# Spare words in front of the activations and the feed-forwards' products in SBUF

## The chip, the cores and the metric

The kernel runs on one core of one Trainium2 chip. The metric is the device time of one execution in microseconds (us), taken over several runs; one further execution is recorded by the hardware profiler, and all rows of the trace come from that one. A difference is called measured here when it is over about 0.2% of the time.

## The reference, cut to what matters

Two transformer blocks follow each other on 256 tokens of width 1024, all in float32. The first block has two layers; each has a feed-forward, a mixer and a second feed-forward:

```python
def swiglu(x, w_gate, w_up, w_down):
    return (jax.nn.silu(x @ w_gate) * (x @ w_up)) @ w_down     # 1024 -> 2816 -> 1024
...
for layer in range(2):
    h = h + 0.5 * swiglu(rms_norm(h, ffn1_norm_g[layer]), ...)
    # layer 0: a convolution of 31 taps beside attention to a memory
    # layer 1: causal attention in 12 heads beside attention to a memory
    h = h + concatenate([primary, mem_out]) @ w_o[layer]
    h = h + 0.5 * swiglu(rms_norm(h, ffn2_norm_g[layer]), ...)
```

The second block has one layer: a projection of 1024 to 6664 columns, differential attention, an mLSTM, two output projections that are gated and added, and a last projection. Most of the work of both is the product of 256 rows with weights that are read once.

## The kernel before, in words

**Precision.** A float32 product is made of three products of a rounded type (fp32r). Each weight tile is split by ACT into a rounded part `whi` (line 1295) and by DVE into the rest `wlo` (line 1897); activations are split in the same way into `xh` and `xl`, and the feed-forward's products into `gh` and `gl`. What is summed is hi by hi, lo by hi and hi by lo.

**Layout.** `B.x` holds two buffers `x0` and `x1`, each [128, 8, 2, 256]: for each of the 8 chunks of the width, 256 tokens of `xh` and behind them 256 tokens of `xl`. `F.g` of the four feed-forwards, `g0` to `g3`, is [128, 22, 2, 256] in the same manner. So one matmul can stream 512 columns, hi and lo, from one chunk.

**Products.** TensorE runs one long program. All matmuls go through the helper `mm` (line 505). In the feed-forwards and most projections a weight tile of 128 by 128 is the stationary operand and the activation moves; `block` makes two matmuls of each:

```python
def block(b, h, l, x, start, stop, ready=None):
    mm(bank[b], h, x.rearrange("p a b -> p (a b)"), start, False)      # 512 columns: hi and lo by whi
    ...
    return mm(bank[b][:, 0:S], l, x[:, 0, :], False, stop)             # 256 columns: hi by wlo
```

`part` and `cols` call it for the gate and up columns, for 8 chunks of `x`; `down` calls it for the 22 chunks of `g`, for 4 pairs of output columns and 2 columns in each: 176 times in each feed-forward. `direct` and `pair` serve the other projections with products of 256 columns alone, from `xh` twice and `xl` once. `rows_steps` turns it round: the activation is stationary, the weights move in 512 columns, or in 512 and 256 where a tile of weights has 768 columns (`w_kv`).

**Order.** Weights pass through 403 slots in an order written out by hand (`weight_plan`). SyncE loads them into 7 buffers `raw`, ACT and DVE split them 4 slots ahead into 5 buffers of `whi` and `wlo`, TensorE takes them in order. The stages are F0 (0 to 220 us of the trace, with the memory's keys and values inside it), mixer A (to 315), F1 (to 525), F2 (to 710), mixer B (to 837), F3 (to 1014), and the second block. F0, F2 and F3 read `x0`, F1 reads `x1`. In each, gate and up columns come first and the 22 chunks of `g` last. ACT copies the right halves of the sums out of PSUM (line 1342) and rounds them (1440); DVE adds, scales and subtracts (1971, 2055, 2063, 2067).

**Where the tensors lie.** Buffers are taken from a stack (`buffers`): those of the whole program first, then each stage's on top, which later stages reuse. In the built program of before they start at these bytes of a partition:

```
raw 16512   whi 45184   wlo 65664   gcol 103552 (256 bytes)
x0 103808   x1 120192   ident 136576   ...   htmp 158528   memt 162624
g0 174912   g1 162624   g2 175392   g3 162624
taps 165696 (840 bytes)   tapp 166560
cs 174912 (128)   posi 175040 (8)   posf 175072 (8)   freq 175104 (32)   ang 175136   rd 175264
```

`g2` lies on top of the keys and values of mixer B (`kT` to `rd`), which F2 must leave alone.

Of the kernel before, what the change touches and what calls it, by code (L numbers as in the profile page):

```python
# [6 lines left out]
F32 = mybir.dt.float32  # L7
# [185 lines left out]
def buffers(nc, ctx):  # L193
# [3 lines left out]
    def sb(name, shape, dt=F32, c=ctx):  # L197
        return c.enter_context(nc.sbuf_tensor(name, shape, dt))
# [9 lines left out]
    B.rowr = sb("rowr", [128, 2, S])  # L208
    B.diag = sb("diag", [128, 2, 128])
    B.gcol = sb("gcol", [128, 8, 8])  # L210
    B.x = [sb(f"x{i}", [128, 8, 2, S], F32R) for i in range(2)]
    B.xh = [x[:, :, 0, :] for x in B.x]
    B.xl = [x[:, :, 1, :] for x in B.x]
    B.ident = sb("ident", [128, 128])
# [15 lines left out]
    def ffn_space(f):  # L230
        c = ExitStack()
        F = Space()
        F.g = sb(f"g{f}", [128, 22, 2, S], F32R, c)
        F.gh, F.gl = F.g[:, :, 0, :], F.g[:, :, 1, :]
        F.gr = sb(f"gr{f}", [128, 2, 512], F32, c)
        F.pr = sb(f"pr{f}", [128, 2, 512], F32, c)
        c.close()
        return F

# [7 lines left out]
    B.xn = sb("xn", [128, 2, D], F32, st0)  # L247
    st0.close()
    F0 = ffn_space(0)

    A = B.a = Space()
# [18 lines left out]
    A.ptbuf = A.gr  # L270
    mx.close()
    F1 = ffn_space(1)

    M = B.b = Space()
# [7 lines left out]
    M.ang = sb("ang", [128, 2, 2, 8], F32, kv)  # L282
    M.rd = sb("rd", [128, 2, 2, 8], F32, kv)
    F2 = ffn_space(2)
    mx = ExitStack()
    M.kn = sb("kn", [128, 2, 768], F32, mx)
# [42 lines left out]
def signals(nc, ctx):  # L329
# [3 lines left out]
    def sig(name, events, by=1):  # L333
        return Signal(ctx.enter_context(nc.semaphore(name)), events, by)
# [55 lines left out]
    s.pe_b = sig("pe_mix_b", [("kT", t, i) for t in T2 for i in T2] + [("qT", t, i) for t in T2 for i in T2])  # L390
    s.pe_c = sig("pe_mix_c", ["ctap", "gt", "F"] + [("xrow", t, j) for t in T2 for j in T2])
    s.zo0 = sig("zo_first_tile", range(3))
# [2514 lines left out]
def program(nc, A, out):  # L2907
    with ExitStack() as ctx:
        B = buffers(nc, ctx)
        B.out = out  # L2910
        B.tap_mem = nc.dram_tensor("tap_mem", (128, 192), F32, kind="Internal").ap()
        B.conv_mem = nc.dram_tensor("conv_mem", (3, 2, 128, 32 + S), F32, kind="Internal").ap()
        s = signals(nc, ctx)
        tensor_engine(nc, B, s)
        scalar_engine(nc, B, A, s)
        vector_engine(nc, B, A, s)
        gpsimd_engine(nc, B, s)
        sync_engine(nc, B, A, s)
# [25 lines left out]
```

## Time and profile before

| | us |
|---|---|
| median of 3 runs | 1244.79 (1244.46 to 1245.52) |
| the profiled execution, its own time | 1244.43 |
| its span, first to last instruction | 1242.9 |
| TensorE busy | 1219.7 |
| DVE busy | 882.6 |
| ACT busy | 681.1 |
| GpSimd busy | 60.6 |

The time of the profiled execution and its span differ by 1.5 us, which lie outside the instructions. Matmuls are pipelined: each lasts longer in the trace than the distance to the next, so the pace is read from starts (first and last start of a row with its count), not from the busy time. A row with 176 matmuls has 175 distances. Where windows cut a stretch, the matmul that is running at the window's edge is counted.

### The profile page before, as it was taken

The page shows a single profiled execution, that of the slowest core. Times are in us where ns is not written, and L with a number is a line of the kernel's source. Part 1 is how long each engine was busy: PE and PEld are TensorE (multiplying, and loading weights), DVE is VectorE, ACT ScalarE, POOL GpSimd, SP SyncE. Part 2 cuts the span into 40 slices and gives each one's busy share as a digit, 9 for nine tenths or more (in the row PEclk, how much of TensorE's full clock was granted, in tenths as well). Part 3 has the DMA queues.
Part 4 walks back from the last instruction along what each step waited for, and adds up shares of the span by engine and source line. Part 5 has one row for each costly group of instructions (what it writes and reads, how often), then busy time and mean ns, then how long its engine had stood idle before and what let it go on. Part 6 is the DMA issues. An engine that isn't in the chain of part 4 may idle for free.

```text
span 1242.9 us, 18893 instructions
## 1 busy us (share of the span) xinstructions
PE 1219.7 (98%) x7518; PEld 1070.2 (86%) x7518; DVE 882.6 (71%) x1256; ACT 681.1 (55%) x1032; POOL 60.6 (5%) x89
## 2 busy tenths in 40 slices
PE   7999999989999999999999999999999999999998
PEld 6888888867888888888888888988888899888996
DVE  6686856785787775777775677577776666666875
ACT  5655544543666554565554456656555455556463
POOL 4000100100010000000000122000000000000000
PEclk9999999999999999999999999999999999999999
DMA  8766556672466655666655555047665566556450
GB/s 273 231 203 193 170 182 191 182 212 51 152 195 195 183 182 178 192 184 195 188 182 185 163 175 188 27 129 212 187 200 171 171 190 188 164 142 180 140 173 34
DMA packets 205653, 215.46 MB, mean 173 GB/s; under 512 B 9808, under 2 KB 192592, under 8 KB 205566
## 3 DMA queue, kind: packets, MB, share of 16 engines
q1 hardware_dynamic: 202998, 210.76, 56.9%
q10 hardware_dynamic: 2568, 3.50, 0.8%
q8 instruction: 60, 0.98, 0.3%
q14 instruction: 27, 0.22, 0.1%
HBM read 212.19 MB, written 2.03 MB: 172 GB/s over the span
## 4 chain that ended last, share of the span: by engine, by line
PE 91%; ACT 3%; DVE 3%; issue 2%; DMA 0%; ACTq 0%; POOL 0%; SPq 0%
PE psum L505 89%; ACT whi L1295 1%; DVE wlo L1897 1%; PE psum L669 0%; PE psum L954 0%; DMA xn<-in_x 0%; ACT qn L1599 0%; PE psum L697 0%; ACT qT L1660 0%; ACT L1736 0%; DVE small L2488 0%; ACT zob L1736 0%; ACT pb L1781 0%; ACTq L1410 0%; DVE small L2334 0%
## 5 line engine op out<-in xcount | busy, mean ns | idle before, releaser
L505 PE MATMUL psum<-x,whi 128*128 128x512 f32 (+1 forms) x2288 | 696.2, 366 | 3.5 <-ACT whi L1295 2.4
L1897 DVE TENSOR_TENSOR wlo<-raw,whi 128x1024 fp32r<-128x1024 f32 (+2 forms) x403 | 474.4, 1190 | 187.8 <-ACT whi L1295 184.4
L505 PE MATMUL psum<-x,wlo 128*128 128x256 f32 x1960 | 550.0, 281 | 1.0 <-DVE wlo L1897 1.0
L1295 ACT CAST whi<-raw 128x1024 fp32r<-128x1024 f32 (+2 forms) x403 | 406.1, 1022 | 165.9 <-PE psum L505 156.6
L505 PEld LDWEIGHTS psum<-x,whi 128*128 128x128 f32 x2288 | 409.8, 189 | 77.3 <-ACT whi L1295 2.8
L505 PEld LDWEIGHTS psum<-x,wlo 128*128 128x128 f32 x1960 | 371.8, 190 | 1.6 <-DVE wlo L1897 1.5
L505 PE MATMUL psum<-g,whi 128*128 128x512 f32 x704 | 247.7, 396 | 0.0
L505 PE MATMUL psum<-g,wlo 128*128 128x256 f32 x704 | 197.9, 281 | 0.0
L505 PEld LDWEIGHTS psum<-g,whi 128*128 128x128 f32 x704 | 132.4, 188 | 31.7
L505 PE MATMUL psum<-whi,x 128*128 128x512 f32 (+1 forms) x512 | 141.2, 376 | 0.1
L505 PEld LDWEIGHTS psum<-g,wlo 128*128 128x128 f32 x704 | 132.2, 188 | 0.0
L505 PEld LDWEIGHTS psum<-whi,x 128*128 128x128 f32 x512 | 90.2, 190 | 16.0 <-ACT zob L1708 0.3
L505 PE MATMUL psum<-wlo,x 128*128 128x512 f32 (+1 forms) x256 | 86.5, 373 | 0.0
L1342 ACT COPY pr<-psum 128x512 f32<-128x512 f32 x44 | 25.8, 586 | 67.1 <-PE psum L505 67.0
L1342 ACT COPY gr<-psum 128x512 f32<-128x512 f32 x44 | 25.7, 585 | 61.1 <-PE psum L505 61.1
L1971 DVE TENSOR_TENSOR pr<-psum,pr 128x512 f32<-128x512 f32 x44 | 30.4, 690 | 35.6 <-ACT pr L1342 35.6
L505 PEld LDWEIGHTS psum<-wlo,x 128*128 128x128 f32 x256 | 46.2, 189 | 8.6
L1372 ACT ACTIVATE x<-hT,gcol 128x256 fp32r<-128x256 f32 x64 | 28.5, 500 | 45.3 <-DVE hT L2106 28.8
L1971 DVE TENSOR_TENSOR gr<-psum,gr 128x512 f32<-128x512 f32 x44 | 30.4, 690 | 31.1 <-ACT gr L1342 31.0
L1989 DVE SCALAR_TENSOR_TENSOR x<-hT,gcol,x 128x256 fp32r<-128x256 f32 x64 | 28.8, 498 | 18.2 <-ACT x L1372 18.2
L1431 ACT ACTIVATE gr<-gr 128x512 f32<-128x512 f32 x44 | 27.6, 632 | 21.3 <-DVE gr L2055 21.2
L1440 ACT CAST g<-pr 128x512 fp32r<-128x512 f32 x44 | 27.4, 623 | 19.3 <-DVE pr L2063 19.3
(322 smaller groups left out, 851.3 us busy)
## 6 DMA issues: line engine op xcount, KB each, us to landing
raw<-in_ffn_w_gate SPq DMA_DIRECT2D x88, 512.0 KB, 4.4
raw<-in_ffn_w_up SPq DMA_DIRECT2D x88, 512.0 KB, 4.1
raw<-in_ffn_w_down SPq DMA_DIRECT2D x80, 512.0 KB, 3.8
raw<-in_w_in SPq DMA_DIRECT2D x52, 512.0 KB, 4.1
raw<-in_w_o SPq DMA_DIRECT2D x16, 512.0 KB, 4.7
raw<-in_a_w_in SPq DMA_DIRECT2D x14, 512.0 KB, 4.7
raw<-in_w_kv SPq DMA_DIRECT2D x16, 384.0 KB, 3.3
raw<-in_w_mem_kv SPq DMA_DIRECT2D x8, 512.0 KB, 3.7
```

Source lines behind the costliest of these rows:

```text
L505: return pe.matmul(o, l, r, start=start, stop=stop, skip_group_check=True)
L1295: act.copy(held(B.whi[:, i % SPLIT, :], *n), held(B.raw[:, i % RAW, :], *n)).then_inc(*s.hi.now(i))
L1342: act.copy(out, psum[:, b:b + 2, S:2 * S]).then_inc(*s.half.now(key))
L1372: act.activation(x[:, c, :], hT[:, c, :], ACT.Copy, scale=gcol[:, c, gi:gi + 1]).then_inc(*s.x_hi.now((gen, c)))
L1431: act.activation(r, r, ACT.Silu).then_inc(*s.silu.now((f, p)))
L1440: act.copy(F.gh[:, 2 * p:2 * p + 2, :], in_pairs(F.pr[:, p % 2, :])).then_inc(*s.g_hi.now((f, p)))
L1897: dve.tensor_tensor(held(B.wlo[:, i % SPLIT, :], *n), held(B.raw[:, i % RAW, :], *n), held(B.whi[:, i % SPLIT, :], *n).bitcast(F32), ALU.s ...
L1971: dve.tensor_tensor(out, psum[:, b:b + 2, 0:S], out, ALU.add).then_inc(*s.sum.now(key))
L1989: dve.scalar_tensor_tensor(out=xl[x][:, c, :], in0=hT[:, c, :], scalar=gcol[:, c, gi:gi + 1], in1=xh[x][:, c, :].bitcast(F32), op0=ALU.mul ...
```

## The change

Two tensors that nothing reads or writes are taken around the two `x` buffers, one of 12 words (48 bytes) in front and one of 4 words (16 bytes) behind, and one of 12 words in front of `g0`, `g1` and `g3`. `g2` gets none. All operations and their order stay.

```diff
@@ buffers
     B.gcol = sb("gcol", [128, 8, 8])
+    sb("lead", [128, 12])
     B.x = [sb(f"x{i}", [128, 8, 2, S], F32R) for i in range(2)]
+    sb("trail", [128, 4])
     B.xh = [x[:, :, 0, :] for x in B.x]
@@ ffn_space
         F = Space()
+        if f != 2:
+            sb(f"lead{f}", [128, 12], F32, c)
         F.g = sb(f"g{f}", [128, 22, 2, S], F32R, c)
```

The change is described as making all of them begin 48 bytes past a multiple of 64.

## Rows read from the trace of the kernel before

**Rows 1.** The page: busy time, granted clock by slice, and the chain that ended last.
```profile
PE 1219.7 (98%) x7518; PEld 1070.2 (86%) x7518; DVE 882.6 (71%) x1256; ACT 681.1 (55%) x1032; POOL 60.6 (5%) x89
...
PEclk9999999999999999999999999999999999999999
...
PE 91%; ACT 3%; DVE 3%; issue 2%; DMA 0%; ACTq 0%; POOL 0%; SPq 0%
PE psum L505 89%; ACT whi L1295 1%; DVE wlo L1897 1%; PE psum L669 0%; PE psum L954 0%; DMA xn<-in_x 0%; ACT qn L1599 0%; PE psum L697 0%; ACT qT L1660 0%; ACT L1736 0%; DVE small L2488 0%; ACT zob L1736 0%; ACT pb L1781 0%; ACTq L1410 0%; 
```

**Rows 2.** Waits of TensorE: us in total, times, longest.
```profile
PE psum L505 <- issue: 4.2, 1, 4.2
PE psum L505 <- ACT whi L1295: 2.4, 1, 2.4
```

**Rows 3.** Groups by form, TensorE: count | busy us, mean ns | idle before.
```profile
L505 PE MATMUL psum<-x,whi 128*128 128x512 f32 x1632 | 576.2, 398 | 3.2 <-ACT whi L1295 2.4 <-DVE pr L1971 0.6 <-DVE x L2362 0.3
L505 PE MATMUL psum<-x,wlo 128*128 128x256 f32 x1960 | 550.0, 281 | 1.0 <-DVE wlo L1897 1.0
L505 PE MATMUL psum<-g,whi 128*128 128x512 f32 x704 | 247.7, 396 | 0.0
...
L505 PE MATMUL psum<-x,whi 128*128 128x256 f32 x656 | 120.1, 285 | 0.2
```

**Rows 4.** Tile g in F0, F1, F2, F3: min/median/max ns, first to last start.
```profile
L505 PE MATMUL psum<-g,whi x176: 392/398/398, 157.5 to 219.3; 128*128 128x512 f32 x176
...
L505 PE MATMUL psum<-g,whi x176: 392/398/398, 462.7 to 524.5; 128*128 128x512 f32 x176
...
L505 PE MATMUL psum<-g,whi x176: 390/392/395, 648.5 to 709.2; 128*128 128x512 f32 x176
...
L505 PE MATMUL psum<-g,whi x176: 389/398/398, 951.6 to 1013.4; 128*128 128x512 f32 x176
```

**Rows 5.** Tile x, six stretches of F0 to F3, the products of 512 columns.
```profile
L505 PE MATMUL psum<-x,whi x35: 392/395/396, 135.8 to 147.6; 128*128 128x512 f32 x35
...
L505 PE MATMUL psum<-x,whi x105: 391/391/392, 354.9 to 391.0; 128*128 128x512 f32 x105
...
L505 PE MATMUL psum<-x,whi x120: 395/398/404, 419.6 to 461.6; 128*128 128x512 f32 x120
...
L505 PE MATMUL psum<-x,whi x11: 395/398/404, 526.6 to 530.2; 128*128 128x512 f32 x11
...
L505 PE MATMUL psum<-x,whi x304: 392/394/396, 542.8 to 647.8; 128*128 128x512 f32 x152
...
L505 PE MATMUL psum<-x,whi x304: 392/394/396, 845.8 to 950.9; 128*128 128x512 f32 x152
```

**Rows 6.** Timeline at F3's entry into its down projection: start us, length us.
```profile
951.23 0.40 PE L505 MATMUL psum<-x,whi 128*128 128x512 f32 x1
...
951.92 0.39 PE L505 MATMUL psum<-g,whi 128*128 128x512 f32 x1
...
952.62 0.40 PE L505 MATMUL psum<-g,whi 128*128 128x512 f32 x1
...
952.98 0.40 PE L505 MATMUL psum<-g,whi 128*128 128x512 f32 x1
```

**Rows 7.** One length alone: timeline of moving weights; tile x from 1046 to 1064 us.
```profile
105.14 0.62 PE L505 MATMUL psum<-whi,x 128*128 128x512 f32 x2
...
105.82 0.62 PE L505 MATMUL psum<-whi,x 128*128 128x512 f32 x2
...
L505 PE MATMUL psum<-x,whi x101: 283/283/284, 1045.8 to 1063.8; 128*128 128x256 f32 x101
L505 PE MATMUL psum<-x,wlo x51: 283/283/284, 1045.9 to 1063.9; 128*128 128x256 f32 x51
```

**Rows 8.** The page: ACT's copies of the sums' halves, and ACT's idle time before them.
```profile
L1342 ACT COPY pr<-psum 128x512 f32<-128x512 f32 x44 | 25.8, 586 | 67.1 <-PE psum L505 67.0
L1342 ACT COPY gr<-psum 128x512 f32<-128x512 f32 x44 | 25.7, 585 | 61.1 <-PE psum L505 61.1
```

## The prediction

> **What bounds the kernel now.** The page's first part and its chain of waits come first: TensorE is busy 98% of the span and its granted clock is at 9 tenths or more in all 40 slices, the level of 2.4 GHz, and the chain runs 91% through TensorE, 89% of it on line 505 [rows 1]. TensorE's own waits then show how little is left to win there: the two longest are 4.2 and 2.4 us, each once [rows 2]. So the time is the pace of the products. The groups by form say which products: 1632 with a moving `x` of 512 columns, and 704 with a moving `g` of 512, each followed by one of 256 columns from the same place with the `wlo` weights [rows 3]. Call a 512 and its 256 a pair.
>
> The change adds and removes no instruction. It can only act through addresses, so the question is whether the pace of a pair hangs on where its moving operand starts. The trace holds the experiment, because `g2` lies at another offset than `g0`, `g1` and `g3`. In all four down projections 176 pairs run without a break. First to last start is 61.8 us for `g0`, `g1` and `g3` (353 ns a pair) and 60.7 us for `g2` (347 ns); the 512s last 398 ns in the first three and 392 in the third [rows 4]. ACT and DVE do the same work in all four, so the offset is the cause I take.
>
> `x` shows both paces from one address. From 420 to 462 us it takes 42.0 us for 119 intervals, 353 ns, with lengths 395/398/404. From 355 to 391 us, and nearly all through F2's and F3's up phases, it takes 347 ns with lengths of at most 396 [rows 5]. The pace changes only after a wait or a norm's small products. So `x`'s offset has a slow and a fast rhythm, and what it was last disturbed by picks one. `g0`, `g1` and `g3` seem to have only the slow one: F3's `x` runs fast up to 951.23, the next two pairs take 0.69 us, two more 0.70 and the one after them 0.36, and the stage stays at 353 [rows 6, 4].
>
> **Where things really land.** In the built program of before every tensor starts on a multiple of 32 bytes, and a shorter one is padded (`taps`, 840 bytes, takes 864; `posi`, 8 bytes, takes 32). Then 48 bytes of `lead` take 64 and 16 bytes of `trail` take 32. `x0` and `x1` move by 64 bytes, all behind them by 96, and `g0`, `g1`, `g3` by 160. None ends 48 past a multiple of 64. I sort by the remainder of 128, since `x` (0) and `g0`, `g1`, `g3` (64) have the same remainder of 64 and yet behave differently:
> - `x`: 0, becomes 64, where `g0`, `g1`, `g3` were.
> - `g0`, `g1`, `g3`: 64, become 96.
> - `g2`: 32, becomes 0, where `x` was.
> - `whi`, `wlo`, `raw`: 0, not moved.
>
> **The sum.** One pair at the slow pace costs 353.1 − 346.7 = about 6.5 ns more [rows 4, 5].
> 1. `x` goes to the offset that knew only the slow rhythm. The pairs that now run fast lose. The three long stretches hold 105, 304 and 304, a shorter one 35 [rows 5]; the rest of the timeline has about 120 more, so 870 in all. 870 × 6.5 = **+5.7 us**.
> 2. `g0`, `g1`, `g3` go to an odd multiple of 32 bytes off the weights, as `g2` is now. The nearest row is `g2`'s. 3 × 176 × 6.5 = **−3.4 us**.
> 3. `g2` goes where `x` was, and comes out of a slow `x` phase. Leaving slow `g1`, `x` took up its slow rhythm at once (lengths 395/398/404 from 526.6 us) [rows 5], so 176 × 6.5 = **+1.1 us**; if it starts fast, 0.
> 4. Products of one length: 512s alone start three in 0.68 us, 227 ns each, and 256s alone 101 and 51 in 18.0 us, 18.0/150 = 120 ns [rows 7]. The fast pair is just their sum, 347, so no row shows a pace below it and a gain is excluded. A loss isn't: the bound is one slow surcharge on two, 984/2 × 6.5 = 3.2 us (656 with `whi` and the half as many with `wlo` [rows 3]). I take 0, the row of today, for nothing alternates in length there. The 96 pairs of 512 and 256 with moving weights in layer 1 keep their moving operand; at most 0.3 us.
> 5. Everything behind `x1` moves by 96 bytes (identity, conv window, heads' operands). That is some 1,100 short products, half of which would move either way: 0, with 2 us either way as an estimate from 6.5 ns on a third of them.
> 6. ACT, DVE and DMA: each sits idle waiting for TensorE, ACT 128 us ahead of the two halves' copies alone [rows 8], so what their operands' offsets do is covered; the cover ends only at the starts of phases, where TensorE's waits are those few us [rows 2].
>
> +5.7 − 3.4 + 1.1 = +3.4 us. The profiled run took 1244.43, 0.4 under the median 1244.79. On the median I forecast **1248.1**; this case's own range is 1245.1 (step 3 at 0, step 5 at −2) to 1253.7 (steps 4 and 5 at their upper ends).
>
> **A page against the rows.** The rows show a contiguous operand at two paces, 392 and 398 ns, by its start [rows 4]. The Trainium skill (SBUF — State Buffer, section Specifications (TRN2)) knows only 16-byte cachelines that want two hits each. All starts here are multiples of 32 before and after, so by that rule the change is worth nothing. It is the fifth rival.
>
> **The rivals.**
> - *x becomes fast (chance 0.17).* The offset of 64 was slow for `g` because it is 64 below the weights' remainder of 256 (64 against 128); `x` will be 64 above (192). If that side is fast, the 760 slow pairs of `x` gain 4.9 us, with −3.4 and +1.1: **1237.5**, on the other side. It decides as soon as fewer than some 1,110 of the 1632 run slow, where the sum passes zero (6.5 ns × (1110 − 762) is the 2.3 us that `g` leaves). For it: F3's entry kept to 0.35 for four pairs. Against: the same remainder of 128 as the slow `g`.
> - *Only the remainder of 64 counts (0.15).* Then `x` keeps both rhythms in the same places and only step 2 and 3 remain: −2.3 to −3.4, **1241.9**. Against: `x` switches to its rhythm with a 404 in it as soon as it follows `g`, and `g` to its even 398, though both have remainder 0 [rows 4, 5].
> - *x slow and g at 96 slow too (0.09).* An offset of 32 is fast, but 96 is as slow as 64: +5.7 + 1.1 = **1251.6**.
> - *The words hold (0.05).* All starts lie 48 past 64 on the chip, nothing else moves, and all pairs are fast as `g2`: −4.9 − 3.4 = **1236.5**. Against: the addresses of the built program.
> - *Nothing (0.04).* The third down stage is fast for another reason than its address: **1244.8**. Against: three stages alike and one apart, each unbroken [rows 4].
>
> **Numbers.** My forecast has 0.50. A measurement of this kernel tells about 0.2%, 2.5 us, from no change. Of the 0.50, where `g2` starts fast the sum is 2.3, so 0.08 is within; slower is 0.42 + 0.09 = 0.51. Within: 0.08 + 0.04 and a third of the second rival, 0.05, which is 0.17. Faster: the other 0.10 of that rival, 0.17 and 0.05, which is 0.32. The range takes in the forecast (less its last 1.2 us, where three bounds would have to meet), the slow rival, no change, the second rival and the start of the first: 1240.0 to 1252.5.
>
> **What would show it.** F0's, F1's and F3's down stages: medians of 392, 60.7 us for 176 pairs; if 398, step 2 is wrong. F2's and F3's `x` between 543 and 648 and between 846 and 951: an even 398 and 353 ns; if 391 to 396, step 1 is wrong and the time falls under 1245. F2's down stage: a 404 among its lengths for the slow rhythm. The 256s of the second block: 120 ns; if more, step 4. TensorE idle growing by more than 1 us would put the cause outside all of this.

## The result and the profile after

The changed kernel takes 1250.58 us in the median of 5 runs (1248.95 to 1252.14) against 1245.52 for the kernel before in 5 runs: +5.1 us, a ratio of 1.004 with a 95% interval of 1.0028 to 1.0051. It is slower, inside the range, and 2.5 us above the forecast of 1248.1. The profiled execution took 1249.65 us, its span is 1248.1 against 1242.9.

The addresses of the built program are those of the prediction: `x0` and `x1` at 64 of 128, `g0`, `g1`, `g3` at 96, `g2` at 0, the weights at 0. No tensor starts 48 past a multiple of 64. All line numbers are 4 higher than before.

The page of the kernel after, the busy times and the chain (first two lines: engine, busy us, share, count; then shares by engine and by line):

```profile
PE 1225.3 (98%) x7518; PEld 1070.9 (86%) x7518; DVE 882.0 (71%) x1256; ACT 680.8 (55%) x1032; POOL 60.6 (5%) x89
...
PE 90%; DVE 4%; ACT 4%; issue 2%; DMA 0%; ACTq 0%; POOL 0%; SPq 0%
```

and TensorE's own waits (us in total, times, longest):

```profile
PE psum L509 <- issue: 4.1, 1, 4.1
PE psum L509 <- ACT whi L1299: 2.4, 1, 2.4
```

TensorE is busy 5.6 us longer [rows 1] and waits no longer [rows 2]; DVE and ACT do not change. So the loss is in the products themselves: in the pace of the long ones and, for 1.6 us of it, in the clock under some short ones (below). Tile `g` in F0, F1, F2 and F3 (count, min/median/max ns, first to last start), which answers to [rows 4]:

```profile
L509 PE MATMUL psum<-g,whi x176: 392/393/394, 158.4 to 219.6; 128*128 128x512 f32 x176
...
L509 PE MATMUL psum<-g,whi x176: 392/394/398, 462.1 to 523.4; 128*128 128x512 f32 x176
...
L509 PE MATMUL psum<-g,whi x176: 392/398/403, 649.4 to 711.3; 128*128 128x512 f32 x176
...
L509 PE MATMUL psum<-g,whi x176: 392/394/398, 957.9 to 1019.1; 128*128 128x512 f32 x176
```

The three that moved to 96 take 61.2 or 61.3 us instead of 61.8, 350 ns a pair; `g2` at 0 takes 61.9 instead of 60.7 and has `x`'s former slow lengths, up to 403. Tile `x` in F1's two parts, in F2 and in F3, which answers to [rows 5]:

```profile
L509 PE MATMUL psum<-x,whi x106: 392/397/398, 353.7 to 390.8; 128*128 128x512 f32 x106
...
L509 PE MATMUL psum<-x,whi x184: 392/392/396, 396.9 to 460.7; 128*128 128x512 f32 x184
...
L509 PE MATMUL psum<-x,whi x298: 392/397/398, 542.7 to 647.7; 128*128 128x512 f32 x149
...
L509 PE MATMUL psum<-x,whi x301: 392/397/398, 850.8 to 956.8; 128*128 128x512 f32 x151
```

F2's and F3's `x` now run at 353 ns ((956.8 − 850.8)/300) where they ran at 347. F1's second part, slow before, runs at 63.8/183 = 349 ns: a rhythm that no row of before had. One length alone, which answers to [rows 7]: moving weights in the timeline (start, length of the merged two), and tile `x` from 1052 to 1066 us:

```profile
105.43 0.63 PE L509 MATMUL psum<-whi,x 128*128 128x512 f32 x2
...
106.14 0.63 PE L509 MATMUL psum<-whi,x 128*128 128x512 f32 x2
...
L509 PE MATMUL psum<-x,whi x81: 279/279/280, 1051.7 to 1065.9; 128*128 128x256 f32 x81
L509 PE MATMUL psum<-x,wlo x41: 279/279/279, 1051.8 to 1066.0; 128*128 128x256 f32 x41
```

Three 512s take 0.70 or 0.71 us instead of 0.68 (233 ns each, 227 before), though their moving weights did not move. The 256s take 14.3 us for 121 distances, 118 ns instead of 120.

Last, the clock. The page's slices are 31 us long, and all 40 still read 9 tenths. Narrow windows tell more. In mixer B TensorE waits 2.2 us for `qn` in the kernel before and 2.1 us in the kernel after; 1.4 us after the end of that wait the granted clock of the kernel after falls to 0.50, the level of 1.2 GHz, from 782.0 to 785.4 us, and in the kernel before it stays at 1.00. These are the windows and the same short products, first before, then after:

```profile
774.00:784.00 10.00, 7.78 (x67) 7.12 (x65) 6.35 (x18) 6.87 (x27) 0.00 (x0) 1.00 0.37 126
...
777.76 1.13 PE L505 MATMUL psum<-kT,qT 128*128 128x256 f32 x4 [2.22 <-ACT qn L1599]
...
779.45 0.83 PE L954 MATMUL psum<-ident,qn 128*128 128x128 f32 x6
780.11 1.45 PE L505 MATMUL psum<-vn,kn 128*128 128x64 f32 x12
```

```profile
782.00:785.40 3.40, 3.40 (x20) 3.34 (x19) 1.94 (x5) 2.06 (x8) 0.00 (x0) 0.50 0.00 0
...
780.62 1.13 PE L509 MATMUL psum<-kT,qT 128*128 128x256 f32 x4 [2.11 <-ACT qn L1603]
...
782.63 1.49 PE L958 MATMUL psum<-ident,qn 128*128 128x128 f32 x6
783.91 2.15 PE L509 MATMUL psum<-vn,kn 128*128 128x64 f32 x12
```

(In a window's row the number before the last two is the granted clock.) The distances between the starts in that stretch add up to 1.6 us more than the same ones before.

The loss by terms. The two traces hold the same 7518 matmuls in the same order, so each distance between two starts can be compared with its own counterpart. The last column is the sum of these differences; the means leave out distances that hold a wait:

| | count | before, ns | after, ns | us |
|---|---|---|---|---|
| pairs of `x` | 1632 | 349.5 | 352.25 | +4.0 |
| pairs of `g0`, `g1`, `g3` | 528 | 353.3 | 350.0 | −1.7 |
| pairs of `g2` | 176 | 346.7 | 353.3 | +1.2 |
| 512s alone, weights moving | 528 | 227.55 | 233.3 | +2.8 |
| 256s alone, `x` moving | 984 | 119.8 | 117.36 | −2.4 |
| 512 and 256 with moving weights | 96 | 349.3 | 353.1 | +0.4 |
| 256s alone, weights moving | 48 | 120 | 114 | −0.3 |
| short products | the rest | | | +1.5 |
| distances with a wait | | | | −0.2 |

Together 5.2 us before rounding, the difference of the spans; the medians differ by 5.1. The paces make +3.9 of it, the short products +1.5. Nearly all of that is the stretch at the lower clock, in which `ident` by `qn` lost 0.6 us, `vn` by `kn` 0.7 and attention's scores the rest.

Such a stretch in mixer B stands in six of the fourteen profiles of this case (after, true48, x32b, x96b, x32g32, wlo64g0) and costs 1.6 or 1.7 us in each. x64, with `x` at the same place as after the change, has none. So it goes with no one address, and what brings it on was not tested. Of the executions that were not profiled only the mean granted clock is known: the changed kernel's slowest, 1252.14 us, has 0.991 and its fastest, 1248.95, has 0.996.

### The profile page after: what moved, and what is told of

Its sections match the earlier page's. It is cut to its first block, busy times and chain, and to the rows that moved or that the text cites. A ratio compares the mean times of both kernels' runs of the same rounds, so it can differ in the third digit from the quotient of the medians.

```text
span 1248.1 us, 18893 instructions
## 1 busy us (share of the span) xinstructions
PE 1225.3 (98%) x7518; PEld 1070.9 (86%) x7518; DVE 882.0 (71%) x1256; ACT 680.8 (55%) x1032; POOL 60.6 (5%) x89
## 4 chain that ended last, share of the span: by engine, by line
PE 90%; DVE 4%; ACT 4%; issue 2%; DMA 0%; ACTq 0%; POOL 0%; SPq 0%
PE psum L509 88%; DVE wlo L1901 1%; ACT whi L1299 1%; PE psum L958 0%; PE psum L673 0%; DMA xn<-in_x 0%; ACT qn L1603 0%; PE psum L701 0%; DVE x L1993 0%; ACT qT L1664 0%; ACT L1740 0%; ACT zob L1740 0%; ACT pb L1785 0%; DVE small L2492 0%; ACTq L1414 0%
```

## The experiments

All start from the kernel before. "At 64" means 64 bytes past a multiple of 128. Where `x` or a weight tile is moved, padding behind it brings all others to 256 bytes further, so that their remainders of 256 stay; where `g` is moved, `gr` and `pr` behind it, which only ACT and DVE use, move with it. The edits of x32b, x96b, g32b and wlo64b were first entered as x32, x96, g32 and wlo64, which left no time and no trace. Theory D: the pace hangs on the difference between the places of the moving and the stationary operand. Rival M: on the moving operand's place alone. The table has all twelve that gave a time, with the kernels before and after above them (mean ns as in the table above; `x` and `g` by feed-forward F0/F1/F2/F3). There is one profile of each, and 4 to 11 executions; each ratio is against executions of the kernel before in the same series, with medians from 1245.08 to 1245.52:

| | x pairs | g pairs | 256s | 512s | median us | ratio to before (95%) |
|---|---|---|---|---|---|---|
| before | 350.5/351.5/347.4/348.1 | 353.3/353.3/346.7/353.2 | 119.8 | 227.6 | 1245.52 | |
| after | 353.1/350.7/353.3/352.6 | 350.0/350.0/353.3/350.1 | 117.4 | 233.3 | 1250.58 | 1.004 (1.0028 to 1.0051) |
| x64 | 351.8/352.4/353.3/353.1 | 353.3/353.2/346.7/353.2 | 117.4 | 233.3 | 1251.42 | 1.0049 (1.0034 to 1.0064) |
| g96 | 350.2/351.3/347.0/348.0 | 350.0/350.0/346.7/350.0 | 119.8 | 227.6 | 1242.58 | 0.9979 (0.997 to 0.9989) |
| all64 | 350.3/351.5/347.4/347.0 | 353.3/353.3/346.7/353.2 | 119.8 | 227.7 | 1244.83 | 0.9997 (0.9987 to 1.0006) |
| true48 | 349.6/352.2/350.1/350.6 | 353.3/353.3/350.0/353.3 | 117.4 | 233.2 | 1248.13 | 1.0023 (1.0013 to 1.0033) |
| x32b | 346.8/346.8/346.8/346.8 | 353.2/353.2/346.7/353.2 | 116.9 | 233.3 | 1242.61 | 0.9977 (0.9967 to 0.9987) |
| x96b | 350.2/350.1/350.0/350.0 | 353.3/353.3/346.7/353.2 | 119.9 | 234.1 | 1250.82 | 1.0043 (1.0028 to 1.0058) |
| g32b | 350.1/351.4/353.0/348.2 | 346.7/346.7/346.8/346.7 | 119.8 | 227.6 | 1244.43 | 0.9993 (0.9983 to 1.0002) |
| wlo64b | 346.9/346.7/346.9/346.7 | 353.3/350.0/353.2/350.0 | 117.9 | 231.5 | 1240.88 | 0.9969 (0.9957 to 0.9981) |
| x32g32 | 346.9/346.8/346.7/346.8 | 346.7/346.7/346.7/346.7 | 116.9 | 233.2 | 1238.57 | 0.9946 (0.9933 to 0.9959) |
| wlo64g0 | 347.1/346.9/346.9/347.0 | 346.7/346.7/346.7/346.7 | 117.8 | 231.7 | 1239.76 | 0.9952 (0.994 to 0.9964) |
| whi64g0 | 349.2/348.3/349.6/348.3 | 340.0/350.0/350.0/350.0 | 118.2 | 232.1 | 1242.09 | 0.9966 (0.995 to 0.9981) |
| xback | 349.9/351.3/347.0/348.2 | 350.0/350.0/346.6/350.0 | 119.9 | 227.6 | 1243.03 | 0.9983 (0.9974 to 0.9992) |

**x64, the activations alone.**

```diff
+    sb("lead", [128, 16])
     B.x = [sb(f"x{i}", [128, 8, 2, S], F32R) for i in range(2)]
+    sb("trail", [128, 48])
```

> The two activation buffers alone start 64 bytes later, everything behind them keeps its remainder of 256. Theory D (what counts is the difference between the places of the moving and of the stationary operand, modulo 128): x pairs at 353 ns in F0, F2 and F3 and 349 in parts of F1; the 512s with moving weights go from 227 to 233 ns though the weights do not move; the 256s alone go from 120 to 117; g pairs stay 353, 353, 347, 353. Time 5.5 to 6 us above before, a little more than the change itself. Rival M (only the moving operand's own place counts): the same for x pairs and 256s, but the 512s with moving weights stay at 227, time +2 to +2.5 us. Rival B (what lies behind x, moved by 96, costs the 512s): 512s at 227 too.

Ratio 1.0049, 6.1 us over before in the medians. The timeline of moving weights in x64:

```profile
105.41 0.63 PE L507 MATMUL psum<-whi,x 128*128 128x512 f32 x2
...
106.11 0.63 PE L507 MATMUL psum<-whi,x 128*128 128x512 f32 x2
```

Three in 0.70 us: the 512s lose with `x` moved alone. `x` is their stationary operand, what lies behind it kept its place, and the weights that stream did not move. Rivals M and B fall for them. A miss in a detail: F1's mean is 352.4, so the rhythm of 349 came up less often than after the change.

**g96, the products alone.**

```diff
+        lead = (40, 40, 0, 40)[f]
+        if lead:
+            sb(f"lead{f}", [128, lead], F32, c)
         F.g = sb(f"g{f}", [128, 22, 2, S], F32R, c)
```

> g0, g1 and g3 alone start 160 bytes later, 96 past a multiple of 128, as in the changed kernel. Both theories: their pairs at 350 ns instead of 353, 176 pairs in each of three stages, 3 x 176 x 3.3 ns = 1.7 us less; every other pace as before. If their 350 came from the x phase ahead of them, they stay at 353 here and the time is that of before.

350.0 to 350.2 in all three stages, and 1242.58: 2.7 us under before by the medians, 1.8 by the spans (1241.1 against 1242.9). The pace of 350 belongs to the place, not to the `x` phase ahead, which was as fast as before.

**all64, everything from the weights on.**

```diff
+    sb("lead_raw", [128, 16])
     B.raw = sb("raw", [128, RAW, SLOT])
```

> Everything from the raw weight buffers on starts 64 bytes later, so all differences between operands stay and all remainders of 128 change. Theory D: every pace as before (x both 353 and 347, g 353, 353, 347, 353, 512s 227, 256s 120), time within 1 us of before. Rival M: x pairs go to 353 and 349 and g0, g1, g3 to the pace of a start at 0, time above before by 3 us or more.

No pace moved and the ratio holds 1. All remainders of 128 changed by 64, all differences stayed. The rows of all64: tile `g` in F1 and F2, tile `x` from 860 to 940 us:

```profile
L506 PE MATMUL psum<-g,whi x176: 396/397/398, 463.1 to 524.9; 128*128 128x512 f32 x176
...
L506 PE MATMUL psum<-g,whi x176: 391/392/395, 648.9 to 709.6; 128*128 128x512 f32 x176
...
L506 PE MATMUL psum<-x,whi x232: 392/394/395, 859.7 to 939.7; 128*128 128x512 f32 x116
```

61.8 and 60.7 us and a fast `x` at 64, the place at which x64 and the changed kernel are slow. Rival M is out; D stands.

One more rival is that TensorE's operands meet the reads and writes of ACT and DVE, whose places all64 moves too. The traces speak against it. In the second block, from 1080 us on, 14 distances between 512s with moving weights fall where ACT and DVE do nothing in the kernel before and average 226.8 ns; 17 in x64 average 233.2. Beside a busy ACT or DVE they are 227.8 and 233.2.

**true48, what the change's description says.** `x0` and `g2` land at 48, `x1`, `g0`, `g1`, `g3` at 112, each 48 past a multiple of 64.

```diff
-    B.x = [sb(f"x{i}", [128, 8, 2, S], F32R) for i in range(2)]
+    B.x = [sb(f"x{i}", [128, 16 + 16 * S], F32R)[:, 12:12 + 16 * S].rearrange("p (k h t) -> p k h t", k=8, h=2)
+           for i in range(2)]
...
-        F.g = sb(f"g{f}", [128, 22, 2, S], F32R, c)
+        at = (12, 12, 4, 12)
+        F.g = sb(f"g{f}", [128, 16 + 44 * S], F32R, c)[:, at[f]:at[f] + 44 * S].rearrange("p (k h t) -> p k h t", k=22, h=2)
```

> The activations and the products are views into longer tensors so that each really starts 48 bytes past a multiple of 64 (x0 and g2 at 48 of 128, x1, g0, g1 and g3 at 112), weights at 0. Theory D has rows only for differences of 32 (347) and 96 (350): I expect pairs between 347 and 350 without a slow rhythm, x pairs gaining 2 to 4 us and g pairs 2 to 3 us, 512s with moving weights between 227 and 233. Time 1239 to 1246. Rival: 48 is a multiple of 16 but not of 32 and costs more than either, time above before.

My expectation failed, the rival's sign holds: 1.0023. At 48 `g2` runs at 350.0, at 112 the other `g` stay at 353.3 and `x1` at 352.2, and the 512s lose as at 64. The profile's span is 5.5 us over, with 1.6 of the lower clock in mixer B in it; the ratio is from all eight executions. So carrying out the words would have cost time too, and the rival of the prediction that gave it 1236.5 is wrong twice.

**x32b and x96b, the activations at 32 and at 96.** As x64, with 8 and 56 words, and with 24 and 40.

> x0 and x1 alone start 32 bytes later (32 past a multiple of 128), all else keeps its remainder of 256. By theory D a pair hangs on the difference alone, and g2 shows 346.7 ns for 32: x pairs at 347 in all four stages without a slow rhythm, 740 pairs gaining 6.6 ns, 4.9 us. For products of one length there is no row at 32; at 64 the 512s lost 5.7 ns and the 256s won 2.4, so between 0 and those: -2.3 to +3.6 us. Time 2 to 7 us below before. If x at 32 still has a slow rhythm, theory D fails for x.

> x0 and x1 alone start 96 bytes later (96 past a multiple of 128). Theory D from g0, g1 and g3 in the changed kernel: x pairs at 350 ns everywhere, against a mean of 349.5 before, so 0 to 1 us more; products of one length unknown between 227 and 233 and between 117 and 120. Time from 1 us under to 4 us over before. If instead x96 behaves as x32, only the remainder of 64 matters once it is not 0.

At 32, tile `x` from 560 to 640 us:

```profile
L507 PE MATMUL psum<-x,whi x232: 390/390/390, 559.8 to 639.8; 128*128 128x512 f32 x116
```

One length, 80.0/231 = 346 ns, in every stage, and no second rhythm. The 256s win 2.9 ns, the 512s lose 5.7. Together 2.7 us under before, the small end of what was expected, since the loss of the 512s was its bad end and the profile holds the stretch at the lower clock, 1.6 us. At 96 the pairs are at 350 as `g` showed, but the 256s win nothing and the 512s lose 6.5: 5.6 us over before, outside the 4 expected. The profile's span is 6.3 over, and distance by distance the 512s with moving weights give 3.0 of it and the short products 2.9. The clock accounts for the latter: 1.6 us in mixer B, and 1.2 in mixer A, where it is at the lower level for 6.8 us (269.3 to 276.1) and in the kernel before for 3.4. The paces alone are near 3, inside what was expected. Whether all four executions, 1250.17 to 1250.90, hold these stretches is not known.

**g32b, the products at 32.** As g96, with leads of (56, 56, 0, 56) words.

> g0, g1 and g3 alone move to 32 past a multiple of 128, where g2 is. Theory D: 346.7 ns in all four down stages, 3 x 176 x 6.6 ns = 3.5 us less than before, 1.8 us less than with g at 96; all other paces as before. If g2 was fast for another reason than its place, the three stay at 353.

All four stages run at 346.7 as expected, yet the time is within noise of before (0.9993). Tile `g` in F1, then tile `x` from 560 to 640 us in F2:

```profile
L508 PE MATMUL psum<-g,whi x176: 391/392/392, 462.8 to 523.5; 128*128 128x512 f32 x176
...
L508 PE MATMUL psum<-x,whi x228: 395/398/403, 559.7 to 639.9; 128*128 128x512 f32 x114
```

`x` was not moved, but F2's `x` phase, fast before (392/394/396 [rows 5]), fell into its slow rhythm, (353.0 − 347.4) × 350 = 2.0 us. Another 1.2 us went in the convolution: its matmuls (`h` by `w`) take 39.5 us from first to last start here and 38.35 before. Here too it is the clock, at the lower level from 268.3 to 275.2 us in g32b and from 271.0 to 274.4 before:

```profile
268.40:275.10 6.70, 5.39 (x52) 2.91 (x56) 3.82 (x9) 1.02 (x4) 0.00 (x0) 0.50 0.92 279
```

3.5 saved, 3.2 given back in this profile: 2.0 by a phase next door that has two rhythms, 1.2 by the clock. Whether the move of `g` brought on either was not tested. The longer stretch at the lower clock also stands in the profiles of xback and x96b.

**wlo64b, one of the two weight tiles.**

```diff
+    sb("lead_lo", [128, 16])
     B.wlo = sb("wlo", [128, SPLIT, SLOT], F32R)
+    sb("trail_lo", [128, 48])
```

> Only wlo moves by 64 bytes; whi, x, g and all else keep their remainders. While a 512 of x runs, a wlo tile is loaded; while its 256 runs, a whi tile. If the load under the 512 sets the pace, g pairs (difference to wlo now 0) get x's old two rhythms, and x pairs those at a difference of 64 (353). If the load under the 256 sets it, all pairs stay as before. The 512s with moving weights have x stationary, so those that stream whi stay at 227 and those that stream wlo go towards 233, 229 on average. Time between 0 and 5 us above before.

Neither of the two simple expectations came. `x` pairs lost their slow rhythm (346.8), `g` pairs are at 353, 350, 353 and 350 (F1 and F3 better, `g2` worse), 512s at 231.5, 256s at 117.9, 4.4 us under before. Tile `x` in F2 and tile `g` in F2 and F3:

```profile
L507 PE MATMUL psum<-x,whi x232: 391/392/393, 559.7 to 639.8; 128*128 128x512 f32 x116
...
L507 PE MATMUL psum<-g,whi x176: 388/397/398, 644.7 to 706.5; 128*128 128x512 f32 x176
...
L507 PE MATMUL psum<-g,whi x176: 390/394/397, 948.7 to 1009.9; 128*128 128x512 f32 x176
```

Since `wlo` alone moved and paces changed, the difference to `wlo` counts. It can't be the only one: `x` lies 64 below `wlo` here and runs at 346.8, and `g` lay 64 below `wlo` before and ran at 353. So a pair's pace hangs on both loads, and there are at least two differences. Which of them sets a pace can't be said from this run.

**x32g32, wlo64g0, whi64g0: can it be made faster?** The first adds x32b and g32b; the second is wlo64b with `g` leads of (16, 16, 24, 16) words, all at 0; the third has the same leads and the two paddings around `whi` instead of `wlo`.

> x0, x1 and all four g at 32 past a multiple of 128, weights at 0. If the paces of the single moves add: all pairs at 346.8 (x 1632, g 704 of them), 256s alone at 117, 512s with moving weights at 233.3. From the x32 run, 2.7 us under before by its times, another 3 x 176 x 6.6 ns = 3.5 us: 6.2 us under before, ratio 0.995.

> wlo alone at 64, and now all four g at 0 of 128, where x lies. The wlo64 run had x pairs at 346.8 without a slow rhythm and g pairs at 353, 350, 353, 350. Theory D: g at x's place takes x's pace, 346.8 in all four stages, 4 x 176 x 4.9 ns = 3.4 us less than that run, which was 4.4 under before: 7.8 us under before, ratio 0.994. If g has a pace of its own whatever its place, it stays at 350 to 353 and the time at 1241.

> The mirror of the kernel before it: whi at 64 and wlo at 0, g at 0. If what frees the pairs is only that the two weight tiles lie 64 apart, x and g pairs are at 346.8 here too and the 512s near 231.5. If the load under the 512 (wlo) decides and wants to be 64 off, pairs keep x's two rhythms as before, 347 to 353, and the time is within 3 us of before or above it.

x32g32 came as added: 1238.57, ratio 0.9946 (6.8 us under before, 12 under the changed kernel), all pairs at 346.8. Its intervals and those of wlo64g0 (0.9952) overlap; both beat both kernels of this case. In wlo64g0 `g` at `x`'s place takes `x`'s pace in all four stages, as D says; the total is 5.6 and not 7.8 us under before. The clock would account for most of what is missing: the profile of wlo64g0 has the stretch in mixer B, 1.7 us, and that of wlo64b has not. x32g32's profile has it as well. whi64g0 is no mirror: `x` at 348 to 350, and tile `g` in F0 and F1:

```profile
L510 PE MATMUL psum<-g,whi x176: 389/389/389, 157.3 to 216.8; 128*128 128x512 f32 x176
...
L510 PE MATMUL psum<-g,whi x176: 393/394/396, 458.7 to 520.0; 128*128 128x512 f32 x176
```

59.5/175 = 340 ns in F0 and 350 in F1, F2 and F3, with the same remainders of 256 of all operands. That is a pace under the 346.7 which I had taken for a floor, and again two rhythms at like places. The seven executions of whi64g0 run from 1236.92 to 1243.99 us, the widest spread of this case; that stages change their rhythm from one execution to the next would explain it, but with one profile it is not shown.

**xback, the change with `x` put back.**

```diff
     B.x = [sb(f"x{i}", [128, 8, 2, S], F32R) for i in range(2)]
+    sb("trail", [128, 24])
...
+        lead = (16, 16, 0, 16)[f]
+        if lead:
+            sb(f"lead{f}", [128, lead], F32, c)
```

> The change with x0 and x1 put back to 0 of 128, and all else where the change has it: g0, g1, g3 at 96, g2 at 0, everything behind x moved by 96. This leaves steps 2, 3 and 5 of the prediction. 512s with moving weights 227.6 and 256s alone 119.8 again; g0, g1, g3 at 350.0, 1.7 us less than before; g2 comes out of a fast x phase into x's own place: 346.8 if it goes on fast, 353.3 and 1.1 us more if not. If the short products' move by 96 costs nothing, the time is 0.5 to 1.8 us below before; if they carried part of the change's loss, it is above before.

1243.03, ratio 0.9983: without the moved `x` the change would gain 2 us. Tile `g` in F2, and the group of moving `whi` by form in xback and in the changed kernel (count, busy us, mean ns):

```profile
L509 PE MATMUL psum<-g,whi x176: 392/394/396, 647.7 to 708.3; 128*128 128x512 f32 x176
...
L509 PE MATMUL psum<-whi,x 128*128 128x512 f32 x416 | 131.5, 398 | 0.1
```

```profile
L509 PE MATMUL psum<-whi,x 128*128 128x512 f32 x416 | 133.6, 403 | 0.1
```

`g2` at 0 runs at 60.6/175 = 346 ns here, coming out of a fast `x`, and at 353 in the changed kernel, coming out of a slow one. The short products kept their move by 96 bytes and cost nothing by it: outside the convolution they differ by less than 0.1 us from before, and the convolution's 0.5 us fall where the clock is at the lower level for 6.8 us instead of 3.4. The span is 1.4 us under before, the paces of `g` alone give 1.7.

## Why the prediction was right, and where it was not

**Placement: right.** Padding to 32 bytes made 48 into 64 and 16 into 32, the addresses of the built program say so, and the paces follow those addresses.

**Sorting by the remainder of 128, not of 64: right in its effect.** x64 moves `x` by 64 bytes alone and costs 0.49%; the rival by which only the remainder of 64 counts is out. But what counts is the difference between operands (all64), and the table is not complete: `g` at 64 never showed the 349 that `x` at 64 has in F1, and whi64g0 has two paces at equal remainders of 256. `g` at 64 is 64 past a multiple of 256 and `x` at 64 is 192 past one, so a remainder of 256 may count there; no run separates it.

**Step 1, `x` goes slow, +5.7: measured +4.0.** F2's and F3's `x` went to 353 as said. The term was too large because `x` at 64 has a second rhythm of 349 that `g` at 64 had not shown, and F1, which had slow pairs to lose, won in it.

**Step 2, `g` to 96, −3.4: measured −1.7.** The nearest row, `g2` at 32, was not near enough: 96 gives 350, halfway. g32b shows that 32 gives the 346.7.

**Step 3, `g2` takes `x`'s slow rhythm, +1.1: measured +1.2**, and its condition (that it comes out of a slow `x`) is borne out by xback, with one profile of each.

**Step 4, products of one length, 0: measured +0.4 (2.8 + 0.4 − 2.4 − 0.3). The reasoning of this step failed, and its small sum is luck.** It took products of one length to be untouched, and priced those with moving weights by the operand that moves alone ("keep their moving operand; at most 0.3 us"). But `x`, their stationary operand, is moved, and the 512s lost 2.8 us by it: 2.8 in x64 too, where `x` alone moves, and less than 0.1 in xback, where it does not. "A gain is excluded" was wrong too: I took the lowest pace seen for the lowest possible. The 256s went to 117.4, and whi64g0 has pairs at 340. The 256s were bounded by a loss of 3.2 us and gained 2.4.

**Step 5, the short products, 0: their move costs nothing**, by xback. Yet they took 1.5 us more in the changed kernel, through the stretch at 1.2 GHz in mixer B. The prediction has no term for the clock: it read 9 tenths in all 40 slices, and such a stretch doesn't show in a slice of 31 us.

**Step 6, the other engines, nothing: right**, by the waits of TensorE, which did not change.

The sum, +3.4, stands against +3.9 from the paces and +5.1 or 5.2 in all. That the paces came so near is in part luck: step 1 was 1.7 us too high and step 2 1.7 us too low, and step 4 hid a loss of 3.2 behind a gain of 2.7. Most of the rest is the clock in the profiled execution.

**The page.** The Trainium skill (SBUF — State Buffer, section Specifications (TRN2)) sets one condition for full bandwidth, two hits in each 16-byte cacheline. All starts here are multiples of 16, so by it all these kernels would tie. The runs span 1238.57 to 1251.42 us with starts at multiples of 32 (and 1248.13 with `x` and `g` at odd multiples of 16). The same page (section Who interferes with whom) lists TensorE's port for the moving operand and the one for LDWEIGHTS as "independent". Here the pace of streaming 512 columns of unmoved weights went from 227 to 233 ns when only the loaded operand moved (x64). The measurement decides. What inside the memory or the engine makes the difference count was not tried and stays open.

## What to carry to other kernels

Where TensorE alternates long and short products with a fresh weight load for each, look at the distance of starts by stage before looking for waits: equal work at two paces is a hint that addresses matter, and moving everything together by 64 bytes against moving one operand tells in two runs whether a place or a difference of places counts. Ask for an offset from the built addresses, not from the sizes in the source, and price every operand that moves in both of its roles, moving and stationary. A stage that has two rhythms at one address can give back a gain made elsewhere, so read the paces of all stages before a small change is called useless. And compare the granted clock of the two traces in windows of a few microseconds before a small difference is put down to the change: here one stretch of 3.4 us at half clock made 1.6 of 5.2 us.

## What the runs showed of the hardware that was not expected

- The pace of matmuls depends on the difference between the start addresses of the streamed and of the loaded operand, at least for differences that are multiples of 16 or 32 bytes: pairs of 512 and 256 columns at 340, 346.7, 349, 350 or 353.3 ns, 512s alone at 227 or 233, 256s alone at 117 or 120. Moving all by 64 changes none of them (all64).
- Like addresses can hold two steady paces: 347 and 353 for `x` in the kernel before, 340 and 350 for `g` in whi64g0. One phase can take either: F2's `x` runs at 347.4 before and at 353.0 in g32b, where it lies at the same place.
- TensorE's granted clock can fall to 1.2 GHz for 3.4 us in one kernel's profile and not in another's with the same instructions and a like wait ahead (2.1 and 2.2 us), for 1.6 us; the page's 40 slices read the same.
- The best place differs by kind: with the weights at 0, `x` at 32 is the best of the places tried for pairs (346.8 everywhere) and for 256s (116.9), and `x` at 0 is the only one with 512s at 227.6.
